# Moving two SBUF regions of matmul operands from 96 to 32 bytes past a multiple of 128

## What is computed

```python
def reference(x, positions, rel_bias, norm_mix, norm_ffn, ...):
    h = x
    for i in range(DEPTH):                      # DEPTH = 2
        a = _rmsnorm(h, norm_mix[i])
        y = _mla(a, ...) if i == 0 else _swa_sinks(a, rel_bias, ...)
        h = h + y
        h = h + _conv_ffn(_rmsnorm(h, norm_ffn[i]), ffn_w_in[i], ffn_conv_w[i], ffn_conv_b[i], ffn_w_out[i])
    return _rmsnorm(h, final_norm)

def _conv_ffn(h, w_in, conv_w, conv_b, w_out):
    u = h @ w_in                                # 2048 -> 11264
    ...                                         # causal convolution of width 3
    gate, val = jnp.split(c, 2, axis=-1)
    return (jax.nn.silu(gate) * val) @ w_out    # 5632 -> 2048
```

## Time and profile before

| | us |
|---|---|
| median of 3 runs | 2039.43 (2038.27 to 2041.24) |
| the profiled execution, its run | 2038.65 |
| its span, first to last instruction | 2036.6 |
| TensorE matmul busy | 2007.4 |
| TensorE weight load busy | 1761.6 |
| VectorE busy | 1433.8 |
| ScalarE busy | 986.5 |
| GpSimd busy | 144.5 |

### The profile page before, as it was taken

How to read it: one execution, slowest core, us unless ns; L and a number is a source line. 1 busy time by engine, 2 the same in 40 slices (tenths; PEclk the granted TensorE clock), 3 DMA queues, 4 the chain that set the end, 5 groups by cost and what they waited for, 6 DMA issues and landing times.

```text
span 2036.6 us, 33814 instructions
## 1 busy us (share of the span) xinstructions
PE 2007.4 (99%) x12008; PEld 1761.6 (86%) x12008; DVE 1433.8 (70%) x1980; ACT 986.5 (48%) x1151; POOL 144.5 (7%) x147
## 2 busy tenths in 40 slices
PE   8899999999999999999999999999999999999998
PEld 7798888888888888888899888888888888888887
DVE  7866777787788777554566668778787777855554
ACT  6456345545544554334445554554555555533332
POOL 1102220000000000110120004100000000001110
PEclk9999999999999999999999999999999999999998
DMA  7457555555555555556575335655556556555553
GB/s 281 145 192 166 176 187 187 195 185 183 197 183 173 191 198 190 186 181 196 188 233 181 125 125 164 198 189 184 177 190 199 186 180 195 182 195 186 187 188 112
DMA packets 103880, 374.46 MB, mean 184 GB/s; under 512 B 11547, under 2 KB 12124, under 8 KB 103548
## 3 DMA queue, kind: packets, MB, share of 16 engines
q1 hardware_dynamic: 101180, 362.55, 53.7%
q0 software_dynamic: 2624, 10.83, 2.1%
HBM read 364.94 MB, written 8.39 MB: 183 GB/s over the span
## 4 chain that ended last, share of the span: by engine, by line
PE 93%; DVE 2%; issue 0%; ACT 0%; DVEq 0%; ACTq 0%
PE ps L409 54%; PE ps L412 27%; PE ps L691 2%; PE ps L692 2%; PE ps L693 2%; PE ps L729 1%; PE ps L740 1%; PE ps L752 1%; DVE w_lo L1103 1%; PE ps L438 1%; PE ps L440 1%; PE ps L439 1%; DVE cv L1118 0%; PE ps L621 0%; PE ps L612 0%
## 5 line engine op out<-in xcount | busy, mean ns | idle before, releaser
L1103 DVE TENSOR_TENSOR w_lo<-raw,w_hi 128x1024 fp32r<-128x1024 f32 (+1 forms) x682 | 832.2, 1231 | 514.5 <-ACT w_hi L822 492.9
L822 ACT ACTIVATE w_hi<-raw 128x1024 fp32r<-128x1024 f32 (+1 forms) x682 | 714.2, 1053 | 816.4 <-PE ps L412 623.4
L409 PE MATMUL ps<-op_in,w_hi 128*128 128x512 f32 x2992 | 1037.8, 394 | 9.5 <-DVE w_lo L1103 9.5
L412 PE MATMUL ps<-op_in,w_lo 128*128 128x256 f32 x2992 | 806.2, 279 | 0.0
L409 PEld LDWEIGHTS ps<-op_in,w_hi 128*128 128x128 f32 x2992 | 549.3, 188 | 126.8 <-issue 8.6
L412 PEld LDWEIGHTS ps<-op_in,w_lo 128*128 128x128 f32 x2992 | 561.6, 188 | 17.3
L409 PE MATMUL ps<-op_ffn,w_hi 128*128 128x512 f32 x1408 | 490.8, 393 | 0.0
L412 PE MATMUL ps<-op_ffn,w_lo 128*128 128x256 f32 x1408 | 387.8, 279 | 0.0
L409 PEld LDWEIGHTS ps<-op_ffn,w_hi 128*128 128x128 f32 x1408 | 261.8, 187 | 60.1
L412 PEld LDWEIGHTS ps<-op_ffn,w_lo 128*128 128x128 f32 x1408 | 263.8, 187 | 2.9
L1612 POOL TENSOR_TENSOR cg<-h 128x1024 f32 (+1 forms) x15 | 43.2, 2882 | 1621.5 <-DVE h L1360 1469.6
(11 more groups left out here) (198 smaller groups left out, 1633.8 us busy)
## 6 DMA issues: line engine op xcount, KB each, us to landing
raw<-weights SPq DMA_DIRECT2D x666, 512.0 KB, 3.4
raw<-weights SPq DMA_DIRECT2D x16, 384.0 KB, 3.1
bias_rows<-brow POOLq DMA_DIRECT2D x1, 6144.0 KB, 36.2
win_bias<-bias_rows POOLq DMA_DIRECT2D x4, 1024.0 KB, 8.2
h<-xt SPq DMA_DIRECT2D x8, 256.0 KB, 7.5
x_tok<-x_rows SPq DMA_DIRECT2D x2, 1024.0 KB, 10.4
y<-yt SPq DMA_DIRECT2D x4, 512.0 KB, 4.0
par<-params SPq DMA_DIRECT2D x1, 352.0 KB, 11.6
```

What stands on the lines that cost most here:

```text
L409: return mm(ps[:, bank, 0:2 * T], whi, op, start=start, stop=stop)
L412: return mm(ps[:, bank, 0:T], wlo, op[:, 0, :], start=False, stop=False)
L822: f(w_hi[s][:, 0:cols], raw[s][:, 0:cols], ACT.Copy).then_inc(hi_ready, 1)
L1103: v.tensor_tensor(w_lo[s][:, 0:cols], raw[s][:, 0:cols], w_hi[s][:, 0:cols].bitcast(F32), ALU.subtract).then_inc(lo_ready, 1)
```

## The change

```diff
-    top[0] = top[0] // 64 * 64 + 96
+    top[0] = (top[0] + 127) // 128 * 128 + 32
     ra = region(KT * 2 * T * 4)
     op_in = place("op_in", [P, KT, 2, T], F32R, ra)
     yt = place("yt", [P, 2, D], F32, ra)
```

## The result

The change makes the kernel faster. Its median is 2019.45 us (2018.73 to 2020.54, 4 runs) against 2038.85 us; the ratio is 0.9903, with a 95% interval of 0.9887 to 0.9919. Between the two profiled executions the span fell from 2036.6 to 2016.7 us, by 19.9 us. The forecast was no change, with a range down to 2027.

A forecast was written before the change was run, and what follows sets the result against it. The prediction took TensorE's matmul pace to bound the kernel. Matmul reads, feeders and DMAs were priced 0 + 0 + 0, so the median was forecast unchanged at 2039.4 us, range 2027 to 2052.

The forecast's parts named there:

- The bound and the multiplier: TensorE's matmul pace sets the end; 11,040 of 12,008 matmuls stream their moving operand from the two moved regions.
- parts 2 and 3: ScalarE's and VectorE's writes of operand halves, and DMAs into or out of the regions: priced 0 each.
- part 1: Moving reads of 11,040 matmuls: the new start costs 0 ns each, bounds 1.1 ns either way, 12.1 us in all.
- same: The forecast itself: median unchanged at 2039.4 us, own range 2035.4 to 2043.5; chance 0.50.
- (b): Plain float32 matmuls (L574, L612, L614): moving starts at remainders 32 and 96 differ by 3 ns at most.
- goes with the length, not the start: Full-rate matmuls: a surcharge of about 6% per column follows the row's length, whichever of the two starts it has.
- Slower: Rival: the change makes the kernel slower; the range takes cases up to 1.1 ns per start, 12 us; chance 0.20.
- Faster: Rival: the change makes the kernel faster; the range takes cases up to 1.1 ns per start, 12 us; chance 0.26.
- Much faster: Rival: the per-column surcharge comes from the start's address; half of 30 ns per pair, 74 us, gives 1965; chance 0.04.
- The independence from what VectorE does: Input and last output products: 287 and 288 matmuls per 50 us although VectorE is busy 39.00 and 25.71 us.

The follow-up runs named there:

- rest64: Kernel before with the weight buffers and all other tiles moved 64 bytes further, the two regions left in place: 2020.54 us, ratio 0.9906.
- wonly64: Kernel before with only w_hi and w_lo moved 64 bytes further modulo 256, everything else unmoved modulo 256: 2020.04 us, ratio 0.9906.
- all192: Kernel before with every tile, weights and regions alike, moved on by 192 bytes: 2039.50 us, ratio 0.9996.
- pair sweep: Kernel before plus test pairs in alternating order, varying moving-to-weights distance and weight columns: 346.7 ns per pair at distance 32, 350.0 at 96.
- turnsweep: Kernel before plus test matmuls strictly in turns, moving starts of the 512 and 256 columns varied separately, also bfloat16: 343.4 to 353.4 ns per pair on the grid.
- shiftsweep: The closer copy: kernel before plus test pairs walking op_ffn in place, weight slices shifted inside w_hi and w_lo; no cell below 340.0 ns per pair.
- hi64: Whole kernel before, relaid so moving operands begin level with w_lo and 64 bytes past w_hi modulo 256: 1994.78 us, ratio 0.9785.
- sweep: Kernel before plus test streams of 24 matmuls at many moving and weight addresses: at distance 96, 256 columns take 120.0 ns.
- r0_r64: Kernel before with op_in at distance 0 and the second region at 64 past the weights: 2044.34 us, ratio 1.0024.

## Why the prediction was wrong

**The bound and the multiplier** were right. TensorE's chain sets the end, 11,040 matmuls count, feeders and DMAs carry nothing of the gain (parts 2 and 3 stay at 0: L835 went from 1063 to 1066 ns, the store of the result has 4.0 us in both), and the pair distance was the row to look at.

**The failed step is the cost of a start in part 1:** 0 ns was taken, with 1.1 ns as bound. It measured -3.4 ns per pair (op_in: 232.3 + 118.2 before, 228.7 + 118.3 after), all of it on the 512 columns, and -3.1 ns per start in narrow_chunk (119.9 to 116.8), some 20 us in all where the sum had 0. Even the full spread of 2.2 ns per 256 columns that the rows showed was too small for the latter. The failure has three parts.

First, I looked for a property of the moving start, and the thing that moved was a distance. The changed kernel's gain can be had with every moving operand on its old byte (rest64), or on its old place modulo 256 (wonly64), and is lost on its new remainder if the weights come along (all192): 2020.54, 2020.04 and 2039.50 us. Comparing starts at 32 and at 96 past a multiple of 128 was about the moving start alone and so missed what changed.

Second, where I did look at the distance, to token_chunk, I took it modulo 128. There the moving weights stand 32 past the stationary operand modulo 128, but 160 modulo 256, and the changed pairs stand at 32. The times repeat after 256 bytes (within 0.2 ns at sixteen distances, pair sweep), so the row was no witness for the new layout. Taken at face value it did not speak for "same" either: its 117.5 and 119.1 ns lie below narrow_chunk's 119.7. I set this aside because two windows of 12 and 11 starts differed by 1.6 ns. Over all starts that difference isn't there, 118.3 ns on op_in (96 starts) and 118.4 on op_lat (191), against 119.9 in narrow_chunk: the spread that I took for noise came from windows too short to average the pattern. (token_chunk's own distance went from 160 to 224 with the change and its time stayed at 118.4.)

Third, (b), the plain float32 matmuls, was read as a sign that addresses don't matter. Plain float32 takes 0.82 ns for a column of four bytes and bfloat16 0.417 for one of two (turnsweep), 4.8 to 4.9 bytes per ns and partition each, where float32r takes 9.0 at 0.4427 ns a column (shiftsweep). The bfloat16 streams don't depend on the distance at the three tried (216 and 109 ns); plain float32 itself was not tried at several distances. So these rows could not bound what the full-rate matmuls do. I had noted that only the full-rate stream pays a surcharge, and still used the half-rate rows as a bound for it. And the surcharge was treated as one thing that "goes with the length, not the start"; 20 of its 30 ns are in every layout tried (340.0 against 320), 10 are not.

**The rivals.** "Slower", 0.20, was the author's guess that the moving stream and the weight loads get in each other's way. No run shows that they meet in the memory; what the runs show is that the distance between the two counts, and the sign for this step was wrong: before was the poorer layout (350.5 ns per pair on op_in, 347.0 after). Nothing in the trace of before could tell the sign, since it holds only one distance per form; that calls for even chances of both signs, not 0.26 against 0.20 beside 0.50 for same. "Faster", 0.26, had the right sign. As a time fixed by the moving start alone it falls (rest64 has the whole gain with every moving start on its old byte), and the 512 and the 256 columns didn't shorten alike either: L409 lost 3.6 to 3.7 ns and L412 none, while narrow_chunk's 256 lost 3.1. "Much faster", the whole surcharge gone, fell for this change, but a third of it was to be had: hi64 has lost 10 of the 30 ns, 45 us.

The range missed by 7.5 us, because its width was the size of the wrong mechanism. The independence from what VectorE does was rightly read, and is confirmed with all engines idle; it doesn't speak for "same", as I had it: the cause lies with TensorE's own two operands (grid of 340.0 to 353.4 ns with no other engine at work).

**What stays open.** Why a distance is good or bad isn't settled. The dependence is on where the moving operand stands to the stationary ones, and it was seen only at the full rate (bfloat16 has 216 and 109 ns at D = 32, 64 and 96 alike); the load records themselves have the same length in all three kernels (187 to 189 ns in the means on op_in and op_ffn: before, changed, hi64). That they collide in the memory isn't shown, and the cut weight loads, which shorten the load (188 to 108 ns) without shortening the pair (346.7 to 349.9 ns), speak against a loss in proportion to what is loaded. Open too is what counts beside the distance, as the sweep's couples at D = 64 and 144 show that something does. That may be why (64, 64) takes 350.0 in the kernel and 352.9 in the copy, in which all operands stand 32 bytes further than in the kernel; it wasn't tested. Last, what made the turn sweep differ at 0, 64 and 224 is open (it used two blocks of the moving operand and four slices, the closer copy forty and three).

## What to carry to other kernels

In a kernel bound by float32r matmuls, the place of the moving operand relative to the stationary one, modulo 256 bytes, is a tuning parameter worth some 2% here (1994.8 against 2039.6 us), with no other cost than a few bytes of padding; find it by trying layouts in the kernel itself or in a block of test matmuls that walks its operands as the kernel does. Give weight sets that take turns their own offsets, and pin both sides, since any tile added ahead of them changes the distance. Before using a row as witness for a new address, ask whether it has the same rate and the same distance in the full period, and average over all its starts: two windows of a dozen differed here by 1.6 ns where the means over all starts differ by 0.1.

## What the runs showed of the hardware

In every layout tried, back-to-back float32r matmuls of 128 x 128 weights take at least 0.443 ns a column in the mean (113.3 ns for 256 in the sweep, 226.9 for 512 in hi64, 340.0 for a pair in shiftsweep), while bfloat16 ones take 109 and 216 ns for 256 and 512 columns, 0.417 ns a column (turnsweep). On top of that comes 0 to 13 ns per pair of 512 and 256 columns on a grid of 32 bytes (340.0 to 353.4, shiftsweep; 20 at D = 16 in the turn sweep, 360.0), with every other engine idle. It depends on the distances of the moving operand to the weights and repeats after 256 bytes within 0.2 ns at all sixteen distances tried (pair sweep). Moving both operands on by 64 or 192 bytes changed nothing (rest64 against the changed kernel, 228.7 and 118.3 ns in both; all192 against before, 287 and 288 matmuls in the same stretches in both, 2039.50 us with a ratio of 0.9996); moving both by 16, 32 or 96 can (sweep, 117.8 against 113.4 ns for 256 columns). Starting everything on a multiple of 128, at distance 0, is among the slow layouts: 352.7 ns per pair in r0_r64. Cutting the weights from 128 to 32 columns shortens the load record from 188 to 108 ns and leaves the pair at 346.7 to 349.9 (pair sweep).
